# Transposing the first block's result in 64-row halves on two row tiles of TensorE

## What is computed

```python
x = first_block(...)        # ends: x = x + conv_ffn(rms_norm(x, ffn_norm_w), ...);  return rms_norm(x, final_norm_w)
# second_block:
h = rms_norm_2(x, norm1_g)
proj = jnp.einsum('bsd,de->bse', h, w_in)
```

## Time and profile before

| what | us |
|---|---|
| median of 3 runs (790.39 to 790.53) | 790.49 |
| the profiled execution | 790.63 |
| its span, first to last instruction | 788.8 |
| TensorE busy in it | 783.5 |
| DVE busy | 594.4 |
| ACT busy | 469.4 |

### The profile page before, as it was taken

The page is one execution under the profiler, slowest core; times in us unless marked ns, Lnnn a source line. Parts: engine busy times, 40 slices in busy tenths (PEclk is TensorE's granted clock), DMA queues, the critical chain, the costliest instruction groups (busy, mean ns, idle before and its releaser), DMA issues.

```text
span 788.8 us, 12561 instructions
## 1 busy us (share of the span) xinstructions
PE 783.5 (99%) x4876; PEld 663.7 (84%) x4876; DVE 594.4 (75%) x977; ACT 469.4 (60%) x673; POOL 4.5 (1%) x16
## 2 busy tenths in 40 slices
PE   9999999999999999999999999999999999999998
PEld 7888889888888888888888888888888888888886
DVE  6996789987778789679988973677776765556654
ACT  6876556655656566887566655656644554434542
POOL 0000000000000000000000000010000000000000
PEclk9999999999999999999999999999999999999999
DMA  9873344664655563736645376333655555665551
GB/s 325 286 256 108 108 160 161 212 207 167 197 185 203 190 240 111 242 131 214 198 142 192 111 246 228 107 93 123 217 179 191 172 186 179 211 206 173 183 183 53
DMA packets 84656, 143.52 MB, mean 182 GB/s; under 512 B 3905, under 2 KB 44673, under 8 KB 84353
## 3 DMA queue, kind: packets, MB, share of 16 engines
q1 hardware_dynamic: 83888, 141.82, 54.4%
q10 hardware_dynamic: 720, 1.05, 0.4%
HBM read 141.29 MB, written 1.05 MB: 180 GB/s over the span
## 4 chain that ended last, share of the span: by engine, by line
PE 95%; DVE 3%; DMA 1%; issue 0%; ACT 0%; ACTq 0%; DVEq 0%
PE bank L539 20%; PE bank L540 20%; PE bank L541 20%; PE bank L628 15%; PE bank L633 8%; PE bank L401 3%; PE bank L1039 2%; PE bank L1041 1%; PE bank L612 1%; PE bank L1180 1%; DMA arena<-in_x_turned 1%; PE bank L1209 1%; DVE w_lo L1902 1%; PE bank L615 0%; PE bank L786 0%; PE bank L1137 0%
## 5 line engine op out<-in xcount | busy, mean ns | idle before, releaser
L1902 DVE TENSOR_TENSOR w_lo<-raw,w_hi 128x1024 fp32r<-128x1024 f32 (+1 forms) x254 | 302.4, 1214 | 53.4 <-ACT w_hi L1351 52.3
L1351 ACT CAST w_hi<-raw 128x1024 fp32r<-128x1024 f32 (+1 forms) x254 | 259.8, 1047 | 121.1 <-PE bank L541 111.2
L539 PE MATMUL bank<-w_hi,h_both 128*128 128x512 f32 x352 | 140.2, 398 | 0.4 <-DVE w_lo L1902 0.4
L540 PE MATMUL bank<-w_lo,h_both 128*128 128x512 f32 x352 | 137.3, 390 | 0.0
L541 PE MATMUL bank<-w_hi,h_both 128*128 128x512 f32 x352 | 137.2, 390 | 0.0
L539 PE MATMUL bank<-w_hi,a_both 128*128 128x512 f32 (+1 forms) x318 | 124.6, 392 | 0.1
L540 PE MATMUL bank<-w_lo,a_both 128*128 128x512 f32 (+1 forms) x318 | 123.5, 388 | 0.0
L541 PE MATMUL bank<-w_hi,a_both 128*128 128x512 f32 (+1 forms) x318 | 123.4, 388 | 0.0
L628 PE MATMUL bank<-a_both,w_hi 128*128 128x512 f32 x512 | 121.5, 389 | 0.0
L628 PEld LDWEIGHTS bank<-a_both,w_hi 128*128 128x128 f32 x512 | 95.5, 188 | 19.4
L539 PEld LDWEIGHTS bank<-w_hi,h_both 128*128 128x128 f32 x352 | 66.2, 188 | 14.7 <-issue 1.8
(11 more groups left out here) (242 smaller groups left out, 885.8 us busy)
## 6 DMA issues: line engine op xcount, KB each, us to landing
raw<-in_w_in SPq DMA_DIRECT2D x45, 1024.0 KB, 5.2
raw<-in_w_up SPq DMA_DIRECT2D x22, 1024.0 KB, 5.1
raw<-in_w_ff_up SPq DMA_DIRECT2D x16, 1024.0 KB, 5.5
raw<-in_w_ff_down SPq DMA_DIRECT2D x16, 1024.0 KB, 5.0
raw<-in_w_down SPq DMA_DIRECT2D x11, 1024.0 KB, 5.0
raw<-in_w_out SPq DMA_DIRECT2D x8, 1024.0 KB, 5.0
raw<-in_w_gla_branch SPq DMA_DIRECT2D x4, 1024.0 KB, 5.1
raw<-in_w_attn_branch SPq DMA_DIRECT2D x2, 1024.0 KB, 5.0
```

Of the source, the lines that this page charges most:

```text
L539: nc.tensor.matmul(dst, l_hi, r_hi, start=start, stop=False)
L540: nc.tensor.matmul(dst, l_hi, r_lo, start=False, stop=False)
L1351: nc.scalar.copy(dst, raw_half(m % RAW, half, size, cols)).then_inc(s.hi_done, 1)
L1902: nc.vector.tensor_tensor(dst, raw_half(n // 2 % RAW, n % 2, size, cols), h, ALU.subtract).then_inc(s.lo_done, 1)
```

## The change

`turn_tile` no longer issues eight 128x128 transposes. A new helper `turn_rows` splits each into two transposes of 64 token rows: rows 0 to 63 and rows 64 to 127 of `x`, each against the matching 64x64 corner of the identity. The two stand in the two row tiles of the array (partitions 0 to 63 and 64 to 127). The first half is written to bank `4 * a`, the second to bank `4 * a + 1`, 64 columns each at the same offset. So a piece of 128 tokens now lies in two banks, where it lay in one, and a bank holds 64 tokens of all eight pieces.

`x_turned` is still raised twice for each tile, but by the last two pieces; ACT's `in2_hi` waits for the second of them in both its halves, and reads each piece as two parts of 64 from two banks. DVE's `in2_lo` waits in both its halves until ACT has done both halves of the tile, and reads the same two banks.

```diff
+            def turn_rows(banks, col, src):
+                for i in range(2):
+                    rows = slice(64 * i, 64 * i + 64)
+                    ins = nc.tensor.transpose(bank[:, banks[i], col:col + 64], src[rows], ident[rows, rows])
+                return ins
...
                 pe.wait_ge(s.x_tiles, 2 + a)
-                for half in range(2):
-                    for k in range(4):
-                        ins = turn(bank[:, 4 * a + half, k * P:(k + 1) * P], x[:, a, (4 * half + k) * P:(4 * half + k + 1) * P])
-                    ins.then_inc(s.x_turned, 1)
+                for k in range(KT):
+                    ins = turn_rows((4 * a, 4 * a + 1), k * 64, x[:, a, k * P:(k + 1) * P])
+                    if k >= KT - 2:
+                        ins.then_inc(s.x_turned, 1)
...
             def in2_hi(a, half):
-                act.wait_ge(s.x_turned, 4 + 2 * a + half + 1)
+                act.wait_ge(s.x_turned, 4 + 2 * a + 2)
                 for k in range(4):
                     t = 4 * half + k
-                    ins = nc.scalar.activation(h_hi[:, t, a * P:(a + 1) * P], bank[:, 4 * a + half, k * P:(k + 1) * P], ACT.Copy,
+                    ins = nc.scalar.activation(h_hi[:, t, a * P:(a + 1) * P].rearrange("p (i t) -> p i t", i=2),
+                                               bank[:, 4 * a:4 * a + 2, t * 64:t * 64 + 64], ACT.Copy,
                                                scale=column("norm1_g_2", t))
...
             def in2_lo(a, half):
-                dve.wait_ge(s.h_hi_done, 7 + 2 * a + half + 1)
+                dve.wait_ge(s.h_hi_done, 7 + 2 * a + 2)
                 for k in range(4):
                     t = 4 * half + k
-                    ins = nc.vector.scalar_tensor_tensor(
-                        h_lo[:, t, a * P:(a + 1) * P], bank[:, 4 * a + half, k * P:(k + 1) * P], column("norm1_g_2", t),
-                        h_hi[:, t, a * P:(a + 1) * P].bitcast(F32), ALU.mult, ALU.subtract)
+                    dst, hi_ = [v[:, t, a * P:(a + 1) * P].rearrange("p (i t) -> p i t", i=2) for v in (h_lo, h_hi)]
+                    ins = nc.vector.scalar_tensor_tensor(dst, bank[:, 4 * a:4 * a + 2, t * 64:t * 64 + 64],
+                                                         column("norm1_g_2", t), hi_.bitcast(F32), ALU.mult, ALU.subtract)
```

## The result

The changed kernel takes **792.18 us** (median of 16 runs, 791.96 to 792.61); the kernel before, run beside it, 790.55 us (790.39 to 790.83). The ratio is 1.0021, with a 95% interval from 1.0014 to 1.0028, so the change costs 1.6 us. The profiled execution took 792.18 us with a span of 790.4 us, at a granted clock of 1.0; before it was 790.63 us with 788.8 us.

A forecast was written before the change was run, and what follows sets the result against it. TensorE, busy 99% of the span, was taken as the bound; its saved 0.14 us is lost before waits of 0.92 and 0.7 us, adding 1.6 us to the median 790.49 us: 792.1 us, range 791.4 to 792.6.

The forecast's parts named there:

- TensorE's own time: Transposes in row tiles: pairs save 0.41 us, switches cost 0.34 us, so TensorE's stream is 0.07 us shorter per tile.
- rivals 1 and 2: Transposes: 1, pairs pass at 0.109 us, 792.5 us, chance 0.16; 2, each half costs 0.109 us, 794.3 us, chance 0.05.
- Tile 0: First token tile: DVE waits for all eight ACT operations, ACT's cast covers the halves; TensorE's load 0.92 us later.
- Tile 1: Second token tile: the same wait exceeds the reserve, adding 0.7 us; TensorE 1.63 us late in all.
- Operands in two banks at no cost: ACT's and DVE's reads of two parts of 64 from two banks: no added time.
- What is late next: After the transposes: DVE's small chain 1.1 us late, the weight split's 0.56 us reserve grows, nothing more lost.
- rival 3: Later waits of TensorE for DVE shrink, leaving 1.0 us of the delay: 791.5 us, chance 0.10.
- rival 4: At the transposes, waits end before TensorE reaches them, so its saved 0.14 us stays: 790.35 us, chance 0.05.

The follow-up runs named there:

- the kernel with four banks for a tile: Changed kernel with each half tile's four pieces in its own bank pair and the old waits by half tile: 792.18 us became 790.57 us, ratio 1.0000 against before.

## Why the prediction was right, point by point

The forecast was 792.1 us in a range from 791.4 to 792.6; it took 792.18. It also gave 0.54 to slower by over 0.2%, which the ratio of 1.0021 meets, though its interval reaches down to 1.0014: it sits on that line, as the prediction said it would. Which side of the line it would fall on was close to an even guess; the mechanism and the 1.6 us were not.

- **TensorE's own time.** Predicted: 0.07 us less for a tile. Measured: from line 541 to the second matmul behind the transposes 294.50 - 293.20 = 1.30 us, against 294.74 - 293.40 = 1.34 with whole transposes under the same waits: 0.04 us. The sum behind the 0.07 has a slip. It prices the way out against a whole transpose's step, which already holds the last of the eight steps, and then counts all eight as saved: with seven, 7 x 0.051 - 0.34 leaves 0.02 us. By the prediction's own parts the stretch is 0.32 + 0.46 + 0.20 + 0.34 = 1.32 us. Measured were 0.32 into the tiles, as forecast, 0.71 - 0.22 = 0.49 from first to last start, then 294.16 - (293.52 + 0.49) = 0.15 and 0.34 on the way out: the pairs took 0.03 us more, the way out 0.05 less. The slip did no harm to the forecast, because this saving lies in front of the waits and is lost there. That the pairs pass together at about 0.06 us, which was a choice between 0.058 and 0.109, held; rivals 1 and 2 fall with it.
- **Tile 0.** Predicted 0.92 us: line 540 moved from 297.51 to 298.35, with the 0.08 us of offset 0.92. ACT's cast covers the halves, as said: ACT starts at 294.58, the offset and 0.01 us away from 294.67.
- **Tile 1.** Predicted 1.63 us in all at line 540, 1.55 if TensorE answers quickly: 305.46 - 303.92 + 0.08 = 1.62 us. Two small errors cancel in it: with the offset, ACT started 0.03 us and DVE 0.04 us later than forecast, and TensorE answered in 0.05 us, not in 0.11 (DVE's fourth operation ends 3 x 0.259 + 0.35 = 1.13 us behind 303.94, at 305.07; the load stands at 305.12).
- **Operands in two banks at no cost**: shown by the kernel with four banks for a tile.
- **What is late next.** DVE's small chain came 306.02 - 304.97 + 0.08 = 1.13 us later (predicted about 1.1). The weight split ends at 308.39 + 1.23 = 309.62, 1.08 us before TensorE's stage, where it had 0.56: the reserve grew, as said. The stage came 1.64 us late and the span 1.6.
- **The delay given back** (rival 3): it was not. The wait of the earlier trace rows is still 0.4 us in the changed kernel.
- **Only TensorE's time counts** (rival 4): this is what happens in tile 1 when the waits by half tile come back, -0.05 us in the seam. There DVE's start behind half of ACT's work is enough, a condition that the rival did not name. In tile 0 the rival's reason held: TensorE waits for DVE, DVE for ACT, and ACT for the end of its cast, so nothing of the saving stays.

## What to carry to other kernels

Look at the granularity at which two engines take turns on a buffer before looking at how fast it is filled: a layout that spreads each piece over all the banks of a tile turns an overlap of ACT and DVE into a sequence, if the two keep off each other's banks as here. In the seam that cost some thirty times what the faster transposes save without it (1.64 against 0.05 us). If pieces have to be split over banks, give each half of the work a set of banks of its own and keep the waits by halves. And a saving on the bound engine counts only if nothing that it next waits for ends later; ask of a faster producer which engine is ready to take its result.

## What the runs showed of the hardware

- Sixteen 64-row float32 transposes in two row tiles pass in pairs. The starts in the changed kernel's trace are 3 to 4 ns apart within a pair; the second pair starts 0.11 us behind the first, each later one about 0.06 us behind the one before it, where whole transposes stand 0.109 us apart.
- Going into row tiles and out again costs 0.30 us around a single pair (the kernel with one of two pieces in halves). In the changed kernel, 0.04 us is left of the 8 x (0.109 - 0.06) = 0.39 us that eight pieces save, so there one excursion takes about 0.35 us.
- The listed duration of a half is no measure of what it costs. It is 0.22 us in the changed kernel (the row below: least, median and most in ns), but 0.27 us in the kernel with one of two pieces in halves, as much as a whole transpose in the earlier trace rows.

```profile
L664 PE MATMUL bank<-ident,x_tok x32: 221/223/272, 293.5 to 301.5; 64*128 64x64 f32 x32
```

- TensorE's answer to the awaited operation of DVE differed: 0.11 us in tile 0, where the code waits for three semaphores, and 0.05 us in tile 1, where it waits for one. No run here separates the number of semaphores from other causes.
